# MoBA attention taken two heads a step, with 64-row score products, and retention's first output chunk ahead of the last pair's values

## The reference

```python
h = rmsnorm(x, norm1_w[l])
rq, rk, rv, rg, mq, mk, mv, ga, gb = jnp.split(h @ w_in[l], split_points, axis=-1)
...
ret = jax.nn.silu(rg) * retention(rq, rk, rv)
a = ret @ w_ret_out[l]
...
b = moba_attention(mq, mk, mv) @ w_moba_out[l]
mix = jax.nn.sigmoid(ga) * a + jax.nn.sigmoid(gb) * b
x = x + mix @ w_o[l]
```

## Time and profile before

| | |
|---|---|
| time, median of 3 runs | 1500.08 us (1499.92 to 1500.76) |
| the profiled execution | 1500.31 us, of which the span from the first to the last instruction is 1498.2 us |
| busy share of TensorE, VectorE, ScalarE, GpSimd | 99%, 62%, 53%, 13% |
| mean granted TensorE clock | 0.998 of full speed |
| MoBA's scores, first to last start | 124.56 us to 162.90 us |

### The profile page before, as it was taken

How to read it: one execution, slowest core, us unless ns; L and a number is a source line. 1 busy time by engine, 2 the same in 40 slices (tenths; PEclk the granted TensorE clock), 3 DMA queues, 4 the chain that set the end, 5 groups by cost and what they waited for, 6 DMA issues and landing times.

```text
span 1498.2 us, 21332 instructions
## 1 busy us (share of the span) xinstructions
PE 1477.7 (99%) x8040; PEld 1275.1 (85%) x8040; DVE 928.7 (62%) x1207; ACT 793.2 (53%) x975; POOL 190.1 (13%) x56
## 2 busy tenths in 40 slices
PE   8999999999999999999999999999999999999997
PEld 6888788888888888888888888888888998888886
DVE  7476455666656665525766668765666565766667
ACT  6436545444444445666544456644446664544456
POOL 0015211000040000372100001000005441100010
PEclk9999999999999999999999999999999999999999
DMA  9545456666546555552565557565555336555562
GB/s 345 185 142 177 135 177 198 217 195 196 186 159 214 184 186 177 187 170 85 196 222 183 186 194 228 176 223 184 186 192 164 124 113 197 196 197 188 184 216 71
DMA packets 187545, 274.73 MB, mean 183 GB/s; under 512 B 10048, under 2 KB 137184, under 8 KB 187488
## 3 DMA queue, kind: packets, MB, share of 16 engines
q1 hardware_dynamic: 183568, 262.77, 53.3%
q10 hardware_dynamic: 3920, 11.18, 2.3%
HBM read 272.83 MB, written 1.05 MB: 183 GB/s over the span
## 4 chain that ended last, share of the span: by engine, by line
PE 91%; DVE 5%; ACT 2%; issue 1%; DMA 0%; DVEq 0%; SPq 0%; ACTq 0%
PE bank L720 23%; PE bank L727 12%; PE acc L584 7%; PE acc L583 7%; PE acc L582 7%; PE bank L582 6%; PE bank L584 6%; PE bank L583 6%; PE bank L766 3%; PE acc L893 2%; PE acc L578 2%; PE bank L629 2%; PE bank L636 2%; PE bank L644 2%; DVE w_lo L1859 1%; PE bank L951 1%
## 5 line engine op out<-in xcount | busy, mean ns | idle before, releaser
L1859 DVE TENSOR_TENSOR w_lo<-w_raw,w_hi 128x2048 fp32r<-128x2048 f32 (+1 forms) x208 | 472.9, 2278 | 165.6 <-ACT w_hi L1410 121.3
L720 PE MATMUL bank<-xT,w_hi 128*128 128x512 f32 x1520 | 361.3, 390 | 0.0
L507 POOL TENSOR_TENSOR w_lo<-w_raw,w_hi 128x2048 fp32r<-128x2048 f32 (+1 forms) x41 | 176.9, 4321 | 1264.9 <-ACT w_hi L1326 1264.9
L720 PEld LDWEIGHTS bank<-xT,w_hi 128*128 128x128 f32 x1520 | 282.6, 188 | 56.6
L1410 ACT ACTIVATE w_hi<-w_raw 128x2048 fp32r<-128x2048 f32 x145 | 276.4, 1906 | 0.0
L1326 ACT ACTIVATE w_hi<-w_raw 128x2048 fp32r<-128x2048 f32 (+4 forms) x105 | 189.4, 1817 | 29.1 <-PE bank L584 10.1
L727 PEld LDWEIGHTS bank<-xT,w_lo 128*128 128x128 f32 x1520 | 189.3, 192 | 3.9
L727 PE MATMUL bank<-xT,w_lo 128*128 128x256 f32 x1520 | 191.4, 284 | 0.0
L582 PE MATMUL acc<-w_hi,sTh 128*128 128x512 f32 x400 | 155.9, 390 | 0.0
L583 PE MATMUL acc<-w_lo,sTh 128*128 128x512 f32 x400 | 155.9, 390 | 0.0
L584 PE MATMUL acc<-w_hi,sTl 128*128 128x512 f32 x400 | 155.8, 390 | 0.0
(11 more groups left out here) (231 smaller groups left out, 2030.0 us busy)
## 6 DMA issues: line engine op xcount, KB each, us to landing
w_raw<-in_ffn_w_in SPq DMA_DIRECT2D x176, 512.0 KB, 4.4
w_raw<-in_ffn_w_out SPq DMA_DIRECT2D x88, 512.0 KB, 4.2
w_raw<-in_w_in SPq DMA_DIRECT2D x52, 512.0 KB, 4.8
w_raw<-in_fox_w_in SPq DMA_DIRECT2D x24, 512.0 KB, 4.6
w_raw<-in_w_ffn_gate SPq DMA_DIRECT2D x22, 512.0 KB, 4.7
w_raw<-in_w_ffn_up SPq DMA_DIRECT2D x22, 512.0 KB, 4.5
w_raw<-in_w_ffn_down SPq DMA_DIRECT2D x22, 512.0 KB, 4.2
w_raw<-in_ple_w_gate SPq DMA_DIRECT2D x16, 512.0 KB, 4.5
```

The source lines that it names most:

```text
L507: pool.tensor_tensor(w_lo[s][:, 0:cols], w_raw[u % RING][:, 0:cols], w_hi[s][:, 0:cols].bitcast(F32), ALU.subtract).then_inc(w_lo_done[u % ...
L720: mm = pe.matmul(bank[b + m], wh[:, k, m], both, start=k == 0 and not narrow_first, stop=k == KD - 1 and narrow_first, skip_group_check=na ...
L1859: nc.vector.tensor_tensor(w_lo[s][:, 0:cols], w_raw[u % RING][:, 0:cols], w_hi[s][:, 0:cols].bitcast(F32), ALU.subtract).then_inc(w_lo_don ...
```

## The change

For MoBA alone (`by_twos`), all three engines that compute go through the steps two heads at a time. On TensorE a step s = 0, 2, ..., 10 is now: `turn(s - 2)`, `lead[s]`, the scores of heads s and s + 1, `turn(s - 1)`, `weigh_pair(s - 4)`, `fill[s]` and `fill[s + 1]`. The scores of the two heads are made by `both_scores`: the same products, each over the head's own 64 rows alone, alternating between rows 0 to 63 (bank 4) and 64 to 127 (bank 5). Both banks are taken at the start. `ret_out0` moves from behind the loop into `fill[9]`, which stands ahead of the last `weigh_pair(6)`; ScalarE's and VectorE's part of it (`ahead("ret_out0")`) moves in the same way. The memory set to zero in `mkz` stays as it is.

```diff
--- before.py
+++ after.py
@@ -530,6 +530,10 @@
 
             return name != "mla"
 
+        def by_twos(name):
+
+            return name in ('moba',)
+
         def weights_T(name, h):
 
             return pair_T[h // 2 % 2 if paired(name) else 0][:, h % 2]
@@ -893,6 +897,17 @@
                             mm = pe.matmul(out, a, b_, start=j == 0, stop=j == len(terms) - 1)
                     mm.then_inc(pe_done, mark("pe_done", "S", name, h))
 
+                def both_scores(h):
+                    for a in range(2):
+                        take(4 + a, ("weights", name, h + a))
+                    for t in range(T):
+                        for a in range(2):
+                            q, k = qk(h + a, t)[0]
+                            rows = slice(64 * a, 64 * a + 64)
+                            mm = pe.matmul(bank[4 + a][:, t * P:t * P + (t + 1) * P], q[rows], k[rows], start=True, stop=True)
+                            if t:
+                                mm.then_inc(pe_done, mark("pe_done", "S", name, h + a))
+
                 def turn(h):
                     need("pe", "weights", name, h)
                     transposes(6, ("pT", name, h), ("PT", name, h),
@@ -916,6 +931,25 @@
                                            weights_T(name, h + a)[:, slice(S, S + P) if t else slice(0, S)],
                                            start=t == 0, stop=t == 1)
                     mm.then_inc(pe_done, mark("pe_done", "PV", name, h + 1))
+
+                for s in range(0, heads + 4, 2) if by_twos(name) else ():
+                    if 2 <= s <= heads:
+                        turn(s - 2)
+                    for work in lead.get(s, ()):
+                        work()
+                    if s < heads and name == "moba":
+                        both_scores(s)
+                    elif s < heads:
+                        scores(s)
+                        scores(s + 1)
+                    if 2 <= s <= heads:
+                        turn(s - 1)
+                    if s >= 4:
+                        weigh_pair(s - 4)
+                    for work in [*fill.get(s, ()), *fill.get(s + 1, ())]:
+                        work()
+                if by_twos(name):
+                    return
 
                 for s in range(heads + 2):
                     if s < heads:
@@ -1028,9 +1062,8 @@
                       {0: [ga0[1]], 1: [ga1[0]], 2: [ga1[1]], 3: [lambda: gb0.run(0)],
                        4: [lambda: gb0.run(1, tiles=(0,)), lambda: to_xT("ret", ro, (0,))],
                        5: [lambda: gb0.run(1, tiles=(1,))],
-                       6: [lambda: to_xT("ret", ro, (1,), b0=2)], 7: [gb1[0]]}, {8: [gb1[1]]})
-            need_xT("ret")
-            chunk("ret_out0", (2, 3), slot0=8)
+                       6: [lambda: to_xT("ret", ro, (1,), b0=2)], 7: [gb1[0]],
+                       9: [lambda: need_xT("ret"), lambda: chunk("ret_out0", (2, 3), slot0=8)]}, {8: [gb1[1]]})
             chunk("ret_out1", (0, 1), slot0=8)
             need("pe", "o", "moba", MOBA_H - 1)
             chunk("moba_out0", (0, 1), src=(sTh, sTl))
@@ -1483,9 +1516,28 @@
                         for t in range(T):
                             note(("xTh", "fox", t, h // 8), "act_done", counts["act_done"])
 
+                def work_of(s):
+                    for work in fill.get(s, ()):
+                        work()
+
+                for s in range(0, heads + 4, 2) if by_twos(name) else ():
+                    if 2 <= s <= heads:
+                        turned(s - 2)
+                    work_of(s - 1)
+                    if s < heads:
+                        exps(s)
+                    if 2 <= s <= heads:
+                        turned(s - 1)
+                    if s >= 4:
+                        keep_o(s - 3)
+                    work_of(s)
+                    if s < heads:
+                        exps(s + 1)
+                if by_twos(name):
+                    return
+
                 for s in range(heads + 3):
-                    for work in fill.get(s - 1, ()):
-                        work()
+                    work_of(s - 1)
                     if s < heads:
                         exps(s)
                     if 1 <= s <= heads:
@@ -1610,8 +1662,8 @@
                        2: [lambda: keep_gate("ga", 1)], 3: [lambda: split_to(unit_at["gb0"][0] + RING)],
                        4: [lambda: xT_evac("ret", (0,), slot0=8)], 5: [lambda: keep_gate("gb", 0)],
                        6: [lambda: xT_evac("ret", (1,), slot0=8, b0=2)],
-                       7: [lambda: split_to(unit_at["gb1"][0] + RING)], 8: [lambda: keep_gate("gb", 1)]})
-            ahead("ret_out0")
+                       7: [lambda: split_to(unit_at["gb1"][0] + RING)], 8: [lambda: keep_gate("gb", 1)],
+                       9: [lambda: ahead("ret_out0")]})
             for stage in ("ret_out1", "moba_out0", "moba_out1"):
                 ahead(stage)
             xT_evac("mix", (0,), slot0=8, b0=4, scale=0.5)
@@ -2107,6 +2159,24 @@
                         for t in range(T):
                             note(("xT", "fox", t, h // 8), "dve_done", counts["dve_done"])
 
+                def work_of(s):
+                    for work in fill.get(s, ()):
+                        work()
+
+                for s in range(0, heads + 4, 2) if by_twos(name) else ():
+                    if s < heads:
+                        soft(s)
+                        soft(s + 1)
+                        weights(s)
+                    work_of(s - 1)
+                    if s >= 4:
+                        rest_o(s - 3)
+                    if s < heads:
+                        weights(s + 1)
+                    work_of(s)
+                if by_twos(name):
+                    return
+
                 for s in range(heads + 3):
                     if s < heads:
                         soft(s)
@@ -2275,8 +2345,8 @@
                     zip((0, 1, 2, 3, 4, 7, 8), [*unit_at["ga0"], *unit_at["ga1"], *unit_at["gb0"], *unit_at["gb1"]][1:])}
             fill[5] = [lambda: xT_evac("ret", (0,), slot0=8)]
             fill[6] = [lambda: xT_evac("ret", (1,), slot0=8, b0=2)]
+            fill[9] = [lambda: ahead("ret_out0")]
             attention("moba", MOBA_H, fill)
-            ahead("ret_out0")
             for n in range(2):
                 ahead(f"ret_out{n}")
                 for t in range(T):
```

## The result

The changed kernel takes 1503.4 us (median of 13 runs, 1502.69 to 1503.97) where the kernel before takes 1500.2 (13 runs, 1499.19 to 1500.76): a ratio of 1.0022, with a 95% interval of 1.0015 to 1.003. The forecast was 1501.3 and no change. The time lies inside the range over all cases, at its upper end (1499.0 to 1503.6), but outside that of the walked-through case alone (1500.4 to 1502.5); some 2 us of loss were not in the sum. The profiled execution took 1503.15 with a span of 1501.0 (before 1500.31 and 1498.2).

The account below looks back on a forecast made before the run. TensorE, busy 99% of the span, bounds the kernel. Scores -1.0, old waits -2.7 and new waits +5.05 sum to +1.25 us (with rounding +1.3) on the 1500.08 median: 1501.3, no change, range 1499.0 to 1503.6.

Parts of the forecast that it names:

- the walked-through case: MoBA stretch followed in time through the new order: +1.25 us, 1501.3, own range 1500.4 to 1502.5, chance 0.64.
- 64-row scores: MoBA score pairs: halves run side by side, 1.06 us instead of 1.32 with switches, 1.0 less in all.
- The rival in which the halves don't overlap: The four score pairs: 1.72 us each instead of 1.06, total +1.7, 1503.0; chance 0.22.
- the estimate of 0.2 more for a pair: Score pairs: at 0.77 of ideal overlap a pair takes some 0.2 us more, giving an estimated 1501.7.
- the wait of gb0: TensorE ahead of gb0's first unit, waiting for GpSimd's low half until 144.05: 0.3 us.
- that of the retention transposes: TensorE ahead of the retention transposes, waiting for bank 2, which ScalarE's first tanh frees: 0.75 us.
- that of ret_out0's second unit: TensorE inside ret_out0's first tile, waiting for the second unit's low half until 182.4: 1.8 us, where 0.20 stood.
- that of gb1: TensorE ahead of gb1, waiting for bank 0, which VectorE frees by low parts behind head 6's weights: 2.05 us.
- The waits of the kernel before: Four TensorE waits in the MoBA stretch and at ret_out0's second unit: all go, 2.7 us less.
- Half covered: ScalarE and VectorE gain on TensorE in the lumps, so half the two long waits goes: 1499.4; chance 0.08.
- the covered case: None of the 5.05 us of new waits is left: 1496.4; chance 0.06.
- a granted clock below full after these waits: Sign against the forecast: TensorE's clock drops behind new waits longer than any before in the stretch; no size given.

Follow-up runs that it names:

- the run with three: Changed kernel with VectorE's low parts ahead of the weights, ret_out0's second unit split in fill 7, and gb0's tanh ahead of the ring's high half on ScalarE: 1496.61 us.
- the run that fills the wait: Changed kernel plus eight unused 512-column products on TensorE, put into the last retention transposes where it waited ahead of gb1: 1501.67 us.
- the run with the earlier unit: Changed kernel with ret_out0's second unit split a step earlier, its high half ahead of the copy of turned head 7 on ScalarE: 1501.39 us.

## Why the prediction was near, and what it missed

**64-row scores: right.** The prediction took 1.06 for a pair with its switches. In the changed kernel a normal product would follow the one of 124.09 at 124.32, and the next ones start at 125.27 and 125.61: 0.95, and 0.11 of a load that nothing covers, 1.06. In the trace's single records the products of the two halves start 6 to 7 ns apart. The rival in which the halves don't overlap falls. So does the estimate of 0.2 more for a pair that the prediction drew from the Trainium skill (TensorE: Matmul & The Clock Gate, Part 3: Packing small matmuls): a pair takes 1.06 here, not 1.26. Weight loads of the changed kernel stand idle for 0.35 ahead of the 64-row ones and for 0.33 behind them, where the prediction had 0.2. That fits what the Trainium skill has in TensorEngine Tiling (Array Packing), Key Properties: a change of tiling mode drains TensorE.

```profile
124.41 0.52 PEld L907 LDWEIGHTS acc<-arena 64*128 64x128 f32 x8 [0.35 <-issue]
125.27 0.19 PEld L586 LDWEIGHTS bank<-w_hi,xT 128*128 128x128 f32 x1 [0.33 <-issue]
```

**Waits: right in place, engine and nearly in size.** On the path the wait of gb0 is 0.45 (143.42, a product behind 143.19, to 143.87) for 0.3; that of the retention transposes 0.69 (from 160.24 + 1.0 for values and switch to 161.93) for 0.75; that of ret_out0's second unit 1.83 (182.00 to 183.83) for 1.8; that of gb1, from the end of eight transposes at 161.93 + 0.87 to 164.95, is 2.15 for 0.15 + 2.05 with bank 3's. The first products of gb0, gb1 and the second unit lose another 0.11 in their load, which the prediction's waits hold as 0.1. gb1 starts 40.54 behind the first scores, in the walk (165.2 less 0.1, from 124.56) as in the trace (124.41 to 164.95). The waits of the kernel before are gone, as said, the last pair's too; they were 2.6 and not 2.7, since 0.39 - 0.23 is 0.16 and not 0.18 for each. Half covered and covered, the rivals on the faster side, did not occur in the change as drawn. Mended orders got there in the run with three, at 1496.61, and the bound of the covered case was 1496.4.

**The step that failed.** It is the term "wait 2.05" ahead of gb1, with the sentence that behind TensorE's waiting instruction everything is queued. It counted the wait for its own length alone: the walk went on from 165.2 with the products of the kernel before, 0.23 apart. They ran 0.43 apart until 168.36, which cost 1.6 by the rows and 1.7 by the run that fills the wait. The prediction names "a granted clock below full after these waits" among the signs against it and gives it neither a price nor a chance. From the first scores to ret_out1's first product it had 67.04 (124.56 to 191.6); the trace has 68.61 (124.41 to 193.02), 1.57 more. With the 1.25 forecast that is 2.82, and the two profiled executions are 2.84 apart (1500.31 and 1503.15), so the traces leave nothing over. The rest of the 3.2 is the place of the two executions beside their medians, 0.11 above and 0.25 below. It was luck that the time lies in the range: the half clock took it out of the range of the case that occurred, and the wide range reaches as far only for the halves that don't overlap, which did not occur.

The rows could have warned. In the earlier trace rows no wait of the stretch is over 0.80, and there the clock was full, so nothing in them priced an idle time of 2 us. The bounds of that term should have run from its own length to its length plus the products at the lower of the two levels.

**What stays open.** Standing idle is the cause, but the length of the last wait alone doesn't decide: 1.67 us of wait near 184 leave the clock full in the changed kernel and in the runs that keep this wait, while in the trace of the run with the earlier unit the clock was at half 1.1 us into the wait of 1.78 (162.53 to 163.6), and in the changed kernel only behind its end. Ahead of the wait of 1.78 TensorE had waited 0.82 for the same transposes, ahead of that of 1.67 it had been busy for 17 us (164.95 to 182). It would fit that both waits count together. No run took the 0.82 away and left the 1.78, so this isn't shown, nor what sets the moment of the fall, nor why the half clock lasted longer in one trace than in the others.

## What to carry to other kernels

When an order is changed, work out each new wait and then ask what the engine that waits does afterwards: here an idle stretch of TensorE, longer than any that the rows of before had there, was paid twice, once as the wait and once as products at half clock. Lumping work by two moved TensorE ahead of its releasers, and a releaser that is late by its place in another engine's stream can be mended by a line or two: here three such edits turned +3.2 us into -3.5. A move that fills an idle engine has to take its inputs along; ret_out0's lost more at its second unit than it filled, and with the unit split a step earlier that wait was gone.

## What the runs showed of the hardware

Two 64-row products in the two halves of the array, each as two float32 records, run side by side (starts 6 to 7 ns apart); the switches in and out cost a pair some 0.4 us of the 0.66 that this saves. The granted clock went to half in or behind an idle stretch with waits of 0.82 and 1.78 us and only eight transposes between them, and stayed there for some 3.4 us in the changed kernel (6.8 in one other trace); eight products in that stretch that nothing used made the kernel faster by 1.7 us.
